# Up weights of an expert in rows of 32 KB, reloaded in one transfer of 4 MB

## The chip, the cores and the metric

The kernel runs on one core of a Trainium2 chip. The metric is the device time of one execution in microseconds; the median of the runs is compared. A profiled execution gives the trace.

## What is computed

Two layers of a diffusion backbone in float32 over 1024 latent tokens and 256 context tokens of width 1024. Layer 0 has neighbourhood attention, layer 1 a bidirectional recurrent block. Each layer ends in a mixture of 32 experts: a router picks 2 of them for every token, and an expert computes

```
hdn = silu(xb @ w1[e]) * (xb @ w3[e])      # w1, w3: 1024 x 512
out = hdn @ w2[e]                          # w2: 512 x 1024
```

Layer 0's experts take all 1280 tokens, layer 1's the 1024 latent ones.

## The kernel before

The change concerns the two expert stages, `experts(0, ...)` and `experts(1, ...)`. The tokens of an expert are cut into items of 32 rows. A **place** is one expert with its items; there are 32 places in an order that mixes full and sparse experts. For every item:

- GpSimd gathers its rows (`gather`, L1697, four buffers `xg`), and VectorE transposes them into `xT` (L1902).
- TensorE does `up` (L1821): 64 matmuls over the chunks 0 to 3 of the expert's weights, which hold w1 and w3.
- ScalarE and VectorE make the hidden rows and transpose them; TensorE does `down` (L1836): 32 matmuls over the chunks 4 and 5, which hold w2.
- ScalarE, or in layer 1 VectorE, moves the result to `y`, and it is stored to `ys_d` from ScalarE's queue (four parts of a buffer).

TensorE's order in a place is `up` of the next item, then `down` of the one before, so at the end of a place the `up` of the next expert's first item stands ahead of the `down` of this expert's last. The last place is done without this overlap.

**Weights.** An expert's weights are six chunks of [128, 2048] float32, 1 MB each, in one of four buffers `wt[b]`, b = place mod 4, 48 KB a partition. The first experts come chunk by chunk (`chunk`, `chunk_at`, L1626, L1631), partly during the stage before. The others are reloads from SP's queue (`reload`, L1643; L1673 for the last buffer's chain): three transfers of 2 MB (L1635), each of two chunks, 128 rows of 16 KB. In HBM, `strips` lays w1 and w3 of an expert out as two blocks of 128 rows of 16 KB and w2 as one.

**Semaphores.** `used[q]` counts the items whose matmuls with chunk q are done. Before a reload of chunks q and q + 1, SP waits for `used[q + 1]` to reach the item count at the end of the place that had the buffer. `w_in[b][q]` tells that a transfer has landed; `arrived` makes TensorE wait for it ahead of chunk 0, 2 and 4 of a place's first item. SP issues in program order, so a wait holds back all issues behind it: the next reload, and after the last one the loads for the merge of the results (L1199, L1464). ScalarE's and GpSimd's transfers have queues of their own, but all queues use the same 16 DMA engines: q1 is SP's, q10 ScalarE's, q0 GpSimd's.

Of the kernel before, what the change touches and what calls it, by code (L numbers as in the profile page):

```python
# [14 lines left out]
P = 128  # L15
D = 1024
# [13 lines left out]
EXPERTS = GROUPS * EPG  # L30
# [6 lines left out]
NCH, CHUNK, WBUF = 6, 2048, 4  # L37
DEEP = 4
SOON = 4
FIXED = WBUF - 1  # L40
# [63 lines left out]
def flat(ap):  # L104
    return ap.rearrange("p a b -> p (a b)")
# [14 lines left out]

def chunk_of(A, l, e, q):

    rows = A["w13"][l, e, q // 2] if q < 4 else A["w2s"][l, e, 0]
    return rows[:, q % 2 * CHUNK:(q % 2 + 1) * CHUNK]


def rows_reversed(ap, rows):
# [4 lines left out]
def program(nc, A, out):  # L132
    root = ExitStack()
    with root:
# [51 lines left out]
        wt = [slot(b)(f"wt{b}", [P, NCH, CHUNK]) for b in range(WBUF)]  # L186
# [631 lines left out]
        class Projection:  # L818
# [72 lines left out]
            def stream(self, sp):  # L891
                l = self.l
                for n in range(2, self.nt):
                    sp.wait_ge(self.sum1_ok, 3 * (n - 2) + 3)
                    self.load_x(sp, n)
                    q = n - 2
                    if q < NCH:
                        view = chunk_of(A, l, 0, q)
                        sp.dma_start(wt[0][:, q, :], view).then_inc(self.w_in[0][q], 16)

                def second(q):
                    view = chunk_of(A, l, 1, q)
                    sp.dma_start(wt[1][:, q, :], view).then_inc(self.w_in[1][q], 16)
# [4 lines left out]
                def third(q):  # L908
                    view = chunk_of(A, l, 2, q)
                    sp.dma_start(wt[2][:, q, :], view).then_inc(self.w_in[2][q], 16)  # L910
# [637 lines left out]
        def experts(l, nt, w_in, merge):  # L1548
# [14 lines left out]
            def T(*shape):  # L1563
# [6 lines left out]
                return ap.rearrange(f"p ({' '.join(names)}) -> p {' '.join(names)}", **dict(zip(names, shape)))  # L1570

            OH, A2, A2c, gl, _, goh, _, _, oh0, oh1, (_, _, _, best0, best1) = scratch(nt)
            in_group = flat(OH[:, 0]).rearrange("p (t g e) -> p t g e", t=nt, g=GROUPS)
            of_group = flat(OH[:, 1])[:, 0:nt * EPG].rearrange("p (t e) -> p t e", t=nt)
            chosen = flat(OH[:, 1])[:, nt * EPG:3 * nt * EPG].rearrange("p (k t e) -> p k t e", k=2, t=nt)
            both = bass.AP(tensor=oh0.tensor, offset=oh0.offset, ap=[list(oh0.ap[0]), [nt * EPG, 2], [EPG, nt], [1, EPG]])
# [24 lines left out]
            used = [nm(f"used{q}") for q in range(NCH)]  # L1601
# [3 lines left out]
            passed, sp_passed = nm("passed"), nm("sp_passed")  # L1605
# [5 lines left out]
            w13v, w2v = A["w13"][l], A["w2s"][l]  # L1611
# [3 lines left out]
            w_in = w_in + [[nm(f"w{FIXED}{q}") for q in range(NCH)]]  # L1615
# [6 lines left out]
            with nc.Block() as block:  # L1622
                @block.sync
                def _(sp):
                    def chunk(e, b, q):
                        sp.dma_start(wt[b][:, q, :], chunk_of(A, l, e, q)).then_inc(w_in[b][q], 16)  # L1626

                    def chunk_at(e, b, q):
                        view = w13v[bass.ds(e, 1), q // 2] if q < 4 else w2v[bass.ds(e, 1), 0]
                        view = view.rearrange("o p c -> (o p) c")[:, q % 2 * CHUNK:(q % 2 + 1) * CHUNK]  # L1630
                        sp.dma_start(wt[b][:, q, :], view).then_inc(w_in[b][q], 16)  # L1631

                    def two_chunks_at(e, b, q):
                        view = w13v[bass.ds(e, 1), q // 2] if q < 4 else w2v[bass.ds(e, 1), 0]
                        sp.dma_start(flat(wt[b][:, q:q + 2, :]), view.rearrange("o p c -> (o p) c")).then_inc(w_in[b][q], 16)  # L1635

                    def reload(r, b):

                        e = sp.value_load(ert[0:1, bass.ds(r, 1)], min_val=0, max_val=EXPERTS - 1)
                        done = sp.value_load(bnd[0:1, bass.ds(r - WBUF + 1, 1)], **span)  # L1640
                        for q in range(0, NCH, 2):
                            sp.wait_ge(used[q + 1], done + (1 if q == NCH - 2 else 0))
                            sp.sem_inc(sp_passed, 1)  # L1643
                            two_chunks_at(e, b, q)

                    for q in Projection.LEFT[l]:
                        chunk(1, 1, q)
                    merge.early_loads(sp)
                    sp.wait_ge(tab_ok, 2)
                    e = sp.value_load(ert[0:1, FIXED:FIXED + 1], min_val=0, max_val=EXPERTS - 1)  # L1650
                    for q in range(4, NCH):
                        chunk_at(e, FIXED, q)
                    sp.wait_ge(e_ok, 1)
                    sp.wait_ge(masks, 4)
                    for q in (2, 3):
                        chunk_at(e, FIXED, q)
                    sp.wait_ge(idx_ok, 2)
                    chunk_at(e, FIXED, 0)
                    sp.wait_ge(masks, 8)
                    chunk_at(e, FIXED, 1)  # L1660
                    sp.wait_ge(tab_ok, 3)
                    with sp.Fori(1, TURNS - 1) as i:
                        for b in range(WBUF):
                            reload(WBUF * i + b, b)
                    for b in range(FIXED):
                        reload(LAST - FIXED + b, b)
                    count = sp.value_load(bnd[0:1, EXPERTS + 2:EXPERTS + 3], min_val=1, max_val=EXPERTS)
                    with sp.Fori(0, count) as k:
                        e = sp.value_load(chain[0:1, bass.ds(k, 1)], min_val=0, max_val=EXPERTS - 1)
                        done = sp.value_load(chain[1:2, bass.ds(k, 1)], **span)  # L1670
                        for q in range(0, NCH, 2):
                            sp.wait_ge(used[q + 1], done + (1 if q == NCH - 2 else 0))
                            sp.sem_inc(sp_passed, 1)  # L1673
                            two_chunks_at(e, FIXED, q)

                    for b, load in enumerate((merge.into_first, merge.into_second, merge.into_third)):
                        r = EXPERTS - WBUF + b + 1
                        done = sp.value_load(bnd[0:1, r:r + 1], **span)
                        sp.wait_ge(used[3], done)
                        sp.sem_inc(sp_passed, 1)  # L1680
                        sp.wait_ge(used[5], done + 1)
                        sp.sem_inc(sp_passed, 1)
                        load(sp)
                    merge.stores(sp)
# [87 lines left out]
                def _(t):  # L1772
# [28 lines left out]
                    def landed(r):  # L1801
                        return past[r % WBUF] + 16 * (r // WBUF) + 16

                    def arrived(b, q, r, more):

                        if q % 2 == 0:
                            t.wait_ge(w_in[b][q], landed(r) if more is None else more + landed(r))
                        elif r < WBUF:
                            t.wait_ge(w_in[b][q], (16 * l if b < FIXED else 0) + 16)
# [501 lines left out]
        def weights_in():  # L2311

            return [[root.enter_context(nc.semaphore(f"w{b}{q}")) for q in range(NCH)] for b in range(FIXED)]

        hT, OT = at("hT", MODS_AT, [P, KD, N]), at("OT", OT_AT, [P, KD, N])
        w_in = weights_in()
# [19 lines left out]
def strips(w1, w3, w2):  # L2336

    up = lambda w: np.asarray(w).reshape(2, EXPERTS, 4, 8, 32, 4, P).transpose(0, 1, 3, 2, 4, 5, 6)
    both = np.stack((up(w1), up(w3)), axis=-2)
    w13 = both.reshape(2, EXPERTS, 2, 4, P, D).transpose(0, 1, 2, 4, 3, 5)  # L2340
    dn = np.asarray(w2).reshape(2, EXPERTS, 4, 4, 32, D).transpose(0, 1, 3, 2, 4, 5)
    w2s = dn.reshape(2, EXPERTS, 1, 4, P, D).transpose(0, 1, 2, 4, 3, 5)
    return {"w13": np.ascontiguousarray(w13).reshape(2, EXPERTS, 2, P, 2 * CHUNK),
            "w2s": np.ascontiguousarray(w2s).reshape(2, EXPERTS, 1, P, 2 * CHUNK)}


# [70 lines left out]
```

## Time and profile before

| | |
|---|---|
| median of 3 runs | 2678.44 us (2677.75 to 2681.88) |
| the profiled execution's own time | 2678.04 us |
| its span, first to last instruction | 2675.9 us |
| TensorE busy (matmul) | 2486.5 us, 93% |
| VectorE, ScalarE, GpSimd busy | 45%, 26%, 17% |
| HBM read, written | 575.27 MB, 61.95 MB |
| mean granted TensorE clock | 0.963 |

Busy shares are averages over stages with different limits. The two expert stages lie at about 1008 to 1513 us and 2135 to 2628 us of the span. A time "from A to B" is in microseconds from the span's start.

### The profile page before, as it was taken

What the parts mean: (1) busy time and instruction counts of PE and PEld (TensorE: products, weight loads), DVE (VectorE), ACT (ScalarE), POOL (GpSimd) and SP (SyncE); (2) the same over time, 40 slices, a digit from 0 to 9 for tenths busy, and PEclk for the clock granted to TensorE, in tenths of its full rate; (3) what the DMA queues carried; (4) which work ended last, traced back from release to release, by engine and by line L of the source; (5) the groups of instructions that cost most, each with busy time, mean ns of one, the idle gap of its engine ahead of it and who ended that gap; (6) DMA issues with size and microseconds to landing.
All of it is one profiled execution on the core that took longest, in us unless ns stands there. A gap on an engine that the chain in (4) does not pass through costs nothing. (4 is left out here: it accounts for less than half of the span.)

```text
span 2675.9 us, 63251 instructions
## 1 busy us (share of the span) xinstructions
PE 2486.5 (93%) x26162; PEld 1781.2 (67%) x26162; DVE 1212.0 (45%) x2794; ACT 690.3 (26%) x1427; POOL 460.8 (17%) x554
## 2 busy tenths in 40 slices
PE   7999999999989969999999679999999699999994
PEld 6887788788854546777777474554545478996552
DVE  3234333333454473222222256565575655554545
ACT  4223222323230002333333364345330000000002
POOL 0012112111122102222222220000011022222222
PEclk9999999999999979999999889999999799999997
DMA  6323223223163469999999761011045799999997
GB/s 272 118 90 122 87 100 119 85 94 125 48 245 120 142 255 408 391 421 420 421 420 421 294 238 32 32 34 45 0 161 202 294 406 420 420 420 421 422 421 285
DMA packets 102664, 633.75 MB, mean 237 GB/s; under 512 B 17016, under 2 KB 29788, under 8 KB 68048
## 3 DMA queue, kind: packets, MB, share of 16 engines
q1 hardware_dynamic: 70768, 539.65, 50.4%
q0 software_dynamic: 17024, 48.27, 4.8%
q10 hardware_dynamic: 14688, 43.08, 4.1%
q8 instruction: 151, 2.47, 0.4%
q14 instruction: 33, 0.27, 0.0%
HBM read 575.27 MB, written 61.95 MB: 238 GB/s over the span
## 5 line engine op out<-in xcount | busy, mean ns | idle before, releaser
L1821 PE MATMUL PS<-wt,xT 128*32 128x256 f32 x11648 | 688.1, 384 | 25.0 <-DMA wt<-in_w 19.0
L1821 PEld LDWEIGHTS PS<-wt,xT 128*32 128x32 f32 x11648 | 494.6, 111 | 173.8 <-issue 27.1
L1836 PE MATMUL PS<-wt,hidT 128*32 128x256 f32 x5824 | 364.4, 382 | 9.5 <-issue 7.5
L1836 PEld LDWEIGHTS PS<-wt,hidT 128*32 128x32 f32 x5824 | 250.7, 111 | 81.9 <-issue 12.2
L731 PE MATMUL PS<-hT,slab 128*128 128x256 f32 x1280 | 295.8, 385 | 6.3 <-DVE low L624 3.5
L1902 DVE STREAM_TRANSPOSE xT<-xg 128x256 f32<-128x256 f32 x186 | 82.8, 445 | 458.2 <-PE PS L1821 450.6
L731 PEld LDWEIGHTS PS<-hT,slab 128*128 128x128 f32 x1280 | 239.7, 192 | 42.8 <-issue 6.5
L444 POOL TENSOR_SCALAR prob<-prob,inv 128x640 f32<-128x640 f32 (+2 forms) x80 | 130.3, 1629 | 661.6 <-DVE inv L639 661.6
L1738 ACT ACTIVATE u<-PS 128x128 f32<-128x128 f32 x186 | 51.7, 278 | 684.1 <-PE PS L1821 670.1
L1697 POOL DMA_INDIRECT xg<-h_d,ib x192 | 198.8, 1035 | 163.8 <-POOL ib L1694 160.4
L522 ACT ACTIVATE prob<-prob,low 128x640 f32<-128x640 f32 (+2 forms) x160 | 117.5, 735 | 300.2 <-DVE low L624 300.2
L624 DVE CUSTOM_DVE_ANT_0 prob<-PS,tab 128x640 f32<-128x640 f32 (+2 forms) x160 | 108.5, 716 | 184.4 <-PE PS L760 178.2
L1746 ACT ACTIVATE y<-PS 32x256 f32<-32x256 f32 x384 | 144.2, 375 | 140.3 <-PE PS L1836 136.8
L736 PE MATMUL PS<-slab,hT 128*128 128x128 f32 x1280 | 151.6, 277 | 0.0
L1923 DVE TENSOR_TENSOR y<-PS,RL 32x256 f32<-32x256 f32 x356 | 148.8, 418 | 5.6
L736 PEld LDWEIGHTS PS<-slab,hT 128*128 128x128 f32 x1280 | 146.4, 192 | 3.9 <-issue 2.4
L940 POOL TENSOR_TENSOR xt_p<-xt_p,bg_p 128x1024 f32<-128x1024 f32 x18 | 44.8, 2495 | 583.7 <-DVE bg_p L982 431.2
L1694 POOL COPY ib<-idx 128x1 int32 (+1 forms) x192 | 35.3, 184 | 635.4 <-DVE xT L1902 599.1
L1078 PE MATMUL PS<-wo,OT 128*128 128x512 f32 x320 | 144.1, 604 | 0.0
L2268 PE MATMUL PS<-uT,wg 128*128 128x512 f32 (+1 forms) x384 | 138.9, 521 | 1.4 <-issue 1.4
L2268 PEld LDWEIGHTS PS<-uT,wg 128*128 128x128 f32 x384 | 72.9, 190 | 69.6 <-issue 66.7
L1914 DVE STREAM_TRANSPOSE hidT<-hid 128x128 f32<-128x128 f32 x184 | 57.4, 312 | 134.4 <-PE PS L1836 133.9
(313 smaller groups left out, 2773.9 us busy)
## 6 DMA issues: line engine op xcount, KB each, us to landing
wt<-in_w SPq DMA_DIRECT2D x112, 2048.0 KB
wt<-in_w2s SPq DMA_DIRECT2D x56, 2048.0 KB
aw<-in_ada_w SPq DMA_DIRECT2D x48, 1024.0 KB, 5.0
wt<-in_w SPq DMA_DIRECT2D x32, 1024.0 KB, 8.3
ys_d<-y ACTq DMA_DIRECT2D x184, 128.0 KB, 6.3
wt<-in_w2s SPq DMA_DIRECT2D x16, 1024.0 KB, 11.9
slab<-in_slabs SPq DMA_DIRECT2D x24, 512.0 KB, 3.4
tab<-in_tables SPq DMA_DIRECT2D x8, 1408.0 KB, 7.2
```

What stands on the lines that cost most here:

```text
L444: g.tensor_scalar(x, x, inv[:, b, 1:2], None, ALU.mult).then_inc(pg_ok, 1)
L522: a.activation(x, x, ACT.Exp, scale=-1.0, bias=low[:, b, j:j + 1], accum_out=sums[:, b, j:j + 1]).then_inc(exp_ok, 1)
L624: v.tensor_tensor_reduce(prob[b][:, j, lo:640], S[j][:, lo:640], tab[h % 2][:, j, at:at + 640 - lo], 1.0, 3e38, ALU.add, ALU.min, low[:, b ...
L731: mm = pe.matmul(W[HALF[n]], slab[m][:, k, :], hT[:, k, c * PW:(c + 1) * PW], start=(k == 0), stop=(k == KD - 1))
L736: mm = pe.matmul(W[HALF[n]][:, o * P:(o + 1) * P], hT[:, k, c * PW + o * P:c * PW + (o + 1) * P], slab[2][:, k, :], start=(k == 0), stop=( ...
L1078: mm = t.matmul(PS[:, self.banks[n % 2] + h, :], self.Z[:, k, n * P:(n + 1) * P], self.wo[:, k, h * 512:(h + 1) * 512], start=(k == 0), st ...
L1697: g.indirect_dma_start(out=xg[j][:, :], out_offset=None, in_=h2v, in_offset=bass.IndirectOffsetOnAxis(ap=ib[:, j:j + 1], axis=0), bounds_c ...
L1746: ins = a.activation(y[rows, q * QD:q * QD + QD], PS[STRIP * q:STRIP * q + STRIP, DOWN, 0:QD], ACT.Copy)
L1821: mm = t.matmul(PS[32 * g:32 * g + 32, UP, 0:QD], xT[:, k * 32:k * 32 + 32], wt[b][:, q, c * 1024 + g * QD:c * 1024 + g * QD + QD], start= ...
L1836: mm = t.matmul(PS[32 * g:32 * g + 32, DOWN, 0:QD], hT_[:, k * 32:k * 32 + 32], wt[b][:, q, c * 1024 + g * QD:c * 1024 + g * QD + QD], sta ...
L1923: ins = v.tensor_tensor(y[rows, q * QD:q * QD + QD], PS[strip, DOWN, 0:QD], merge.gate[strip, :], ALU.mult)
L2268: mm = t.matmul(dst[:, c:c + wd], wg[:, q, k, o * P:(o + 1) * P], uT[k][:, c:c + wd], start=(k == 0), stop=(k == 1))
```

## The change

`strips` lays w1 and w3 of an expert out as one block of 128 rows of 32 KB. A reload has two transfers: chunks 0 to 3 in one of 4 MB (`up_at`), issued when `used[3]` has reached the count, and chunks 4 and 5 in one of 2 MB (`down_at`), as before. TensorE waits for a landing ahead of chunk 0 and chunk 4 only (`arrived`); the first loads into a buffer keep a transfer and a wait for each chunk, now with rows of 8 KB out of rows of 32 KB. The same bytes are moved.

```diff
--- before.py
+++ after.py
@@ -120,8 +120,8 @@
 
 def chunk_of(A, l, e, q):
 
-    rows = A["w13"][l, e, q // 2] if q < 4 else A["w2s"][l, e, 0]
-    return rows[:, q % 2 * CHUNK:(q % 2 + 1) * CHUNK]
+    rows, first = (A["w13"][l, e, 0], 0) if q < 4 else (A["w2s"][l, e, 0], 4)
+    return rows[:, (q - first) * CHUNK:(q - first + 1) * CHUNK]
 
 
 def rows_reversed(ap, rows):
@@ -1626,22 +1626,28 @@
                         sp.dma_start(wt[b][:, q, :], chunk_of(A, l, e, q)).then_inc(w_in[b][q], 16)
 
                     def chunk_at(e, b, q):
-                        view = w13v[bass.ds(e, 1), q // 2] if q < 4 else w2v[bass.ds(e, 1), 0]
-                        view = view.rearrange("o p c -> (o p) c")[:, q % 2 * CHUNK:(q % 2 + 1) * CHUNK]
+                        view, first = (w13v[bass.ds(e, 1), 0], 0) if q < 4 else (w2v[bass.ds(e, 1), 0], 4)
+                        view = view.rearrange("o p c -> (o p) c")[:, (q - first) * CHUNK:(q - first + 1) * CHUNK]
                         sp.dma_start(wt[b][:, q, :], view).then_inc(w_in[b][q], 16)
 
-                    def two_chunks_at(e, b, q):
-                        view = w13v[bass.ds(e, 1), q // 2] if q < 4 else w2v[bass.ds(e, 1), 0]
-                        sp.dma_start(flat(wt[b][:, q:q + 2, :]), view.rearrange("o p c -> (o p) c")).then_inc(w_in[b][q], 16)
+                    def up_at(e, b):
+                        view = w13v[bass.ds(e, 1), 0]
+                        sp.dma_start(flat(wt[b][:, 0:4, :]), view.rearrange("o p c -> (o p) c")).then_inc(w_in[b][0], 16)
+
+                    def down_at(e, b):
+                        view = w2v[bass.ds(e, 1), 0]
+                        sp.dma_start(flat(wt[b][:, 4:6, :]), view.rearrange("o p c -> (o p) c")).then_inc(w_in[b][4], 16)
 
                     def reload(r, b):
 
                         e = sp.value_load(ert[0:1, bass.ds(r, 1)], min_val=0, max_val=EXPERTS - 1)
                         done = sp.value_load(bnd[0:1, bass.ds(r - WBUF + 1, 1)], **span)
-                        for q in range(0, NCH, 2):
-                            sp.wait_ge(used[q + 1], done + (1 if q == NCH - 2 else 0))
-                            sp.sem_inc(sp_passed, 1)
-                            two_chunks_at(e, b, q)
+                        sp.wait_ge(used[3], done)
+                        sp.sem_inc(sp_passed, 1)
+                        up_at(e, b)
+                        sp.wait_ge(used[5], done + 1)
+                        sp.sem_inc(sp_passed, 1)
+                        down_at(e, b)
 
                     for q in Projection.LEFT[l]:
                         chunk(1, 1, q)
@@ -1668,10 +1674,12 @@
                     with sp.Fori(0, count) as k:
                         e = sp.value_load(chain[0:1, bass.ds(k, 1)], min_val=0, max_val=EXPERTS - 1)
                         done = sp.value_load(chain[1:2, bass.ds(k, 1)], **span)
-                        for q in range(0, NCH, 2):
-                            sp.wait_ge(used[q + 1], done + (1 if q == NCH - 2 else 0))
-                            sp.sem_inc(sp_passed, 1)
-                            two_chunks_at(e, FIXED, q)
+                        sp.wait_ge(used[3], done)
+                        sp.sem_inc(sp_passed, 1)
+                        up_at(e, FIXED)
+                        sp.wait_ge(used[5], done + 1)
+                        sp.sem_inc(sp_passed, 1)
+                        down_at(e, FIXED)
 
                     for b, load in enumerate((merge.into_first, merge.into_second, merge.into_third)):
                         r = EXPERTS - WBUF + b + 1
@@ -1803,7 +1811,7 @@
 
                     def arrived(b, q, r, more):
 
-                        if q % 2 == 0:
+                        if q % 4 == 0:
                             t.wait_ge(w_in[b][q], landed(r) if more is None else more + landed(r))
                         elif r < WBUF:
                             t.wait_ge(w_in[b][q], (16 * l if b < FIXED else 0) + 16)
@@ -2337,10 +2345,10 @@
 
     up = lambda w: np.asarray(w).reshape(2, EXPERTS, 4, 8, 32, 4, P).transpose(0, 1, 3, 2, 4, 5, 6)
     both = np.stack((up(w1), up(w3)), axis=-2)
-    w13 = both.reshape(2, EXPERTS, 2, 4, P, D).transpose(0, 1, 2, 4, 3, 5)
+    w13 = both.reshape(2, EXPERTS, 1, 8, P, D).transpose(0, 1, 2, 4, 3, 5)
     dn = np.asarray(w2).reshape(2, EXPERTS, 4, 4, 32, D).transpose(0, 1, 3, 2, 4, 5)
     w2s = dn.reshape(2, EXPERTS, 1, 4, P, D).transpose(0, 1, 2, 4, 3, 5)
-    return {"w13": np.ascontiguousarray(w13).reshape(2, EXPERTS, 2, P, 2 * CHUNK),
+    return {"w13": np.ascontiguousarray(w13).reshape(2, EXPERTS, 1, P, 4 * CHUNK),
             "w2s": np.ascontiguousarray(w2s).reshape(2, EXPERTS, 1, P, 2 * CHUNK)}
```

## Rows read from the trace of the kernel before

**Rows 1.** The page's 40 equal slices of the span, 66.9 us each

```profile
PE   7999999999989969999999679999999699999994
DMA  6323223223163469999999761011045799999997
```

**Rows 2.** Windows of 50 us in the two expert stages, with the columns' names

```profile
core 0: us, PE busy (x) PEld busy (x) DVE busy (x) ACT busy (x) POOL busy (x), PEclk, DMA share, GB/s
1150.00:1200.00 50.00, 50.00 (x936) 39.95 (x931) 12.18 (x40) 17.15 (x49) 11.97 (x20) 1.00 1.01 420
2300.00:2350.00 50.00, 50.00 (x934) 45.05 (x927) 28.83 (x78) 2.78 (x10) 11.14 (x19) 1.00 1.01 420
2550.00:2600.00 50.00, 44.89 (x764) 25.01 (x760) 23.89 (x64) 2.22 (x8) 9.74 (x16) 0.90 1.01 422
```

**Rows 3.** Waits (us, times, longest): TensorE 2150 to 2600, VectorE 1030 to 1480

```profile
PE PS L1821 <- DMA wt<-in_w: 19.0, 7, 4.2
...
DVE xT L1902 <- PE PS L1821: 270.3, 87, 3.2
```

**Rows 4.** The page's DMA issues of the whole execution

```profile
wt<-in_w SPq DMA_DIRECT2D x112, 2048.0 KB
wt<-in_w2s SPq DMA_DIRECT2D x56, 2048.0 KB
...
ys_d<-y ACTq DMA_DIRECT2D x184, 128.0 KB, 6.3
```

**Rows 5.** Timeline of SP's queue in layer 1's expert stage (start us, us)

```profile
2127.67 12.69 SPq L1631 DMA_DIRECT2D wt<-in_w  x4
2143.82 2.07 SPq L1635 DMA_DIRECT2D wt<-in_w  x2
...
2222.63 2.05 SPq L1635 DMA_DIRECT2D wt<-in_w  x2
```

**Rows 6.** Timeline of TensorE in layer 1's expert stage

```profile
2141.61 3.66 PE L1821 MATMUL PS<-wt,xT 128*32 128x256 f32 x64 [1.52 <-DVE hid L1910]
...
2570.53 1.91 PE L1836 MATMUL PS<-wt,hidT 128*32 128x256 f32 x32
2575.89 3.64 PE L1821 MATMUL PS<-wt,xT 128*32 128x256 f32 x32 [3.44 <-DMA wt<-in_w]
2581.20 3.64 PE L1821 MATMUL PS<-wt,xT 128*32 128x256 f32 x32 [1.67 <-DMA wt<-in_w]
2584.61 2.15 PE L1836 MATMUL PS<-wt,hidT 128*32 128x256 f32 x32
...
2617.27 4.65 PE L1821 MATMUL PS<-wt,xT 128*32 128x256 f32 x64
```

**Rows 7.** The chain of waits between 2400 and 2620

```profile
2538.30 42.85 DMA wt<-in_w
```

**Rows 8.** Windows of single stretches, columns as in rows 2

```profile
1106.00:1108.00 2.00, 2.00 (x44) 1.57 (x37) 0.28 (x1) 1.47 (x4) 0.83 (x1) 1.00 0.07 17
...
2145.00:2146.00 1.00, 1.00 (x28) 0.71 (x21) 0.61 (x2) 0.28 (x1) 0.04 (x1) 1.00 0.68 131
...
2581.20:2584.60 3.40, 3.40 (x32) 1.57 (x36) 0.00 (x0) 0.00 (x0) 0.00 (x0) 0.50 1.00 424
```

**Rows 9.** DMA queues, 1137 to 1460: packets, MB, share of 16 engines

```profile
q1 hardware_dynamic: 8256, 120.15, 88.3%
q10 hardware_dynamic: 3011, 8.25, 6.5%
q0 software_dynamic: 3002, 7.06, 5.7%
```

**Rows 10.** DMA queue of SP, 1107.8 to 1460 and 2143.8 to 2581.2

```profile
q1 hardware_dynamic: 8955, 130.54, 88.1%
...
q1 hardware_dynamic: 11289, 164.14, 89.3%
```

## The prediction

> **What bounds the kernel now.** I read the page's slices first [rows 1]: the 16 DMA engines are full in two stretches, slices 15 to 21 and 30 to 39, where TensorE is full too. These are the two expert stages, 28 reloads of 6 MB and some 90 items each. The windows part them [rows 2]. In layer 0 (1150 to 1200) TensorE is busy 50.00 of 50.00 us at full clock; the DMA engines are full as well, but nobody waits. In layer 1, 2300 to 2350 looks the same, yet 2550 to 2600 has TensorE at 44.89 of 50 us, clock 0.90, with the DMA still full. The waits name the loads [rows 3]: seven times, 19.0 us. So layer 0 is paced by TensorE, while layer 1 is paced by weight transfers until its last stall, and by TensorE from there to the end.
>
> That last stall is the hinge. TensorE finishes a `down` begun at 2570.53, gets the first 2 MB of the next expert at 2575.89, the second at 2581.20, and never waits for weights again [rows 6]. The chain of waits shows that the second transfer was issued 42.85 us before it landed [rows 7]: the queue is then far behind its issues, so when SP issues it doesn't matter, only how fast the queue moves. Counting from the first reload at 2143.82 [rows 5], the two halves are the ups of the 26th reload, 78 - 1 = 77 transfers of 2.097 MB = 161.5 MB.
>
> **The change part by part.** The sum is made against the profiled execution's 2678.04 us (span 2675.9 and 2.1 around it), 0.4 us under the median run.
>
> *Packets.* A weight transfer is 128 rows of 16 KB. With rows of 32 KB, the up weights need 128 packets fewer, and one set of 16 completions fewer: 144 packets an expert, 9 per engine. What does a packet cost besides its bytes? Two queues with different packet sizes over the same 323 us of 16 engines (5168 engine-us) [rows 9]: q1 has 8256 packets, 120.15 MB, 88.3% = 4563 us; q10 has 3011 packets, 8.25 MB, 6.5% = 336 us. With time = a x packets + b x bytes these give b = 0.0373 us per KB (thousand bytes) and a = 9.2 ns (8.2 to 10.3 within the rounding of 6.5%). Nine packets x 9.2 ns = 0.083 us an expert, and x 26 experts until the hinge **-2.2 us**. Bounds: 0, if a row of 32 KB is still moved as two packets; -4.4, twice the estimate, because q10 writes to HBM and q1 reads, so the fit is coarse.
>
> The Trainium skill ("DMA: Bandwidth & Descriptors", section on why small descriptors are slow) gives a fixed cost of some 3 cycles per packet and calls merging worth it only at small sizes; the trace's 9.2 ns has the same sign, and the rule by itself would make this term nearly nothing, the case without a gain below.
>
> *The first issue comes later.* Before, the first half of the reload waits for used[1], half of a place's last `up`; now all of it waits for used[3], the end. An `up` is 64 matmuls in 3.66 us, so this is 1.8 us later. Queued behind it on SP is only the down reload, whose own wait is later still. Where the queue has work this costs nothing: the sixth reload of layer 1 is issued at 2222.63 [rows 5], when q1 still has to move what is left of five reloads; the queue moves 0.375 MB per us [rows 10], so 31.5 MB issued from 2143.8 last until about 2228, and 1.8 us fit into the 5. But at the stage's start nothing is queued: SP issues the first reload at 2143.82, the previous load (1 MB) was issued about 2140, the first item's `up` began at 2141.61, and in 2145 to 2146 the DMA share is 0.68 [rows 8]. All of the 1.8 us is then lost to a stage paced by the queue: **+1.8 us** (bounds 0, if the gap was there anyway, and 2.0).
>
> *The wait at the hinge is coarser.* Before, half of the `up` was done when the second 2 MB landed; the rest took 2581.20 to 2584.61, 3.4 us, at the low clock (0.50) [rows 6, 8]. Now 64 matmuls start at that landing. At the low clock throughout they take 6.8 us; if the clock returns after the 3.4 us in which it was low before, the other half takes 1.7 us. Hence +1.7 to +3.4. TensorE has now been idle since 2572.4 without the half `up` in between, but at 2584.61 the clock was back 3.4 us after the resumption, so I take the near end: **+1.8 us**. The earlier stalls get the same delay and hide it: TensorE then arrives later at the next stall, which ends by the queue's time. Behind the hinge the next weights are early: the last expert's `up` at 2617.27 waits for no load [rows 6].
>
> *Layer 0.* The queue runs dry once, at 1106 to 1108 (share 0.07) [rows 8], since TensorE frees the buffers late; there the reload now starts 1.8 us later too. Does TensorE ever wait because of it? The tightest place is late in the stage: 21 reloads after the gap, an `up` begins at 1468.21, and its 4 MB are complete when 20 x 6.29 + 4.19 = 130.0 MB have moved since 1107.8. The queue has moved 130.5 MB at 1460 [rows 10]. The slowest of 16 engines lags the mean: at the hinge, 164.1 MB had moved for 161.5 MB needed (plus at most 1.0 MB left from before), 1.6 to 2.6 MB, 4 to 7 us. So the margin is 1 to 4 us; 1.8 us later and 21 x 0.083 = 1.7 us quicker leaves it. **0** (bound: +2 where it is just gone).
>
> *Others' transfers.* The gathers of rows and the stores of results share the engines with weights: q0 and q10 have about 3000 packets for 63 items, 48 an item, 3 per engine [rows 9]. If each waits for one whole weight packet, now 1.22 us in place of 0.61 (32.8 and 16.4 thousand bytes at b), an item's three take 3 x 1.22 and some own time, about 4.5 us, under the item's 5.18 us. The store takes 6.3 us to land [rows 4]; + 3 x 0.61 = 8.1 us, and its buffer is wanted again four items, 20 us, later. DVE has never waited for a gather [rows 3]. Cost nothing; without that cover, see the rivals. SP's fewer instructions and TensorE's fewer waits: nothing, neither is waited for.
>
> The sum: -2.2 + 1.8 + 1.8 + 0 = **+1.4 us**, 2679.4 against the profiled 2678.04, and **2679.8 us** against the median. All terms at their low bounds: -4.4 + 0 + 1.7 = -2.7, 2675.7. All high: 0 + 2.0 + 3.4 + 2 = +7.4, 2685.8.
>
> **Rivals.** *No gain from packets.* A row of 32 KB is cut in two, or a packet's fixed part overlaps its bytes: +1.8 + 1.8 = +3.6, 2682.0. For it: the DMA share is 1.01 and 420 GB/s with rows of 16 KB already, with little room above. Against it: the fit's 9.2 ns.
>
> *Slower: long rows move more slowly.* The 16 engines read rows 32 KB apart in place of 16 KB, and each holds on to a row for 1.22 us; if that costs 2% of the rate, 26 reloads x 16.8 us (437.4 us from first issue to hinge / 26) = 437 us give 8.7 us more in layer 1, and in layer 0 21 x 16.8 x 2% = 7.1 us against a margin of about 2.5 us, some 5 us. With +3.6 this is +17, 2696. It decides (over 0.2%, 5.4 us) from 0.4% on. Against it: rows of 16 KB flow at the same 420 GB/s in every window. The Trainium skill ("DMA: Bandwidth & Descriptors", the row on HBM row pitch in "Latency and other measured facts") has the rate falling with large power-of-two pitches, 207 in place of 214 GB/s at 512 KB, and says nothing as low as 32 KB; by 3% everywhere the same sum would be +23.
>
> *Slower: gathers late.* If small packets wait for two weight packets each, 3 x 2.44 = 7.3 us an item exceeds 5.18, and some 140 items in full-queue stretches x 2.1 us are +300 us. It decides from 1.7 us of waiting per packet. Against it: the store's 6.3 us, about what three single turns and a landing need.
>
> *Faster: the laggard catches up.* A transfer lands with its slowest engine, 4 to 7 us behind the mean at the hinge. If fewer, longer packets halve that (3 us), the sum is -1.6, 2676.8; with the large packet gain -3.8 or, with no loss at the start, -5.6, 2672.8. Nothing in the profile says why an engine lags, so it may as well grow.
>
> **How the numbers follow.** Forecast 0.55, no gain from packets 0.18, long rows slower 0.13 (a third of it under 0.4%), gathers late 0.02, laggard 0.12 (two thirds still within the bound). 0.2%, 5.4 us, is about what a measurement of this kernel tells from no change. Faster 0.06 (0.04 from the laggard, 0.02 from the forecast's own low side), slower 0.13 (0.09 long rows, 0.02 gathers, 0.02 high sums), same 0.81; the laggard growing takes 0.03 more to slower and the unexpected 0.02 to faster: 0.08, 0.76, 0.16. The range takes in the bounds 2675.7 and 2685.8, the laggard's side down to 2674 and part of the slower rival, up to 2687.
>
> **What would show it.** Right: 56 issues of 4096 KB; q1's packets fewer by 56 x 144 = 8064; stalls on `up` of layer 1 with 64 matmuls behind one landing; the last stall ending at 2581 + 1.8 - 2.2, near 2581; TensorE in layer 0 still without a wait; stores landing in about 8 us. Wrong: an unchanged packet count (no gain), GB/s under 417 in full windows or a hinge after 2587 (long rows, laggard), DVE waiting for gathers, or a first gap in layer 1 that doesn't widen.

## The result, and the profile after

The changed kernel takes 2683.11 us (median of 20 runs, 2676.52 to 2687.82), the kernel before, on the same chip, 2677.37 (20 runs, 2674.16 to 2683.26). The ratio is 1.0019, with a 95% interval from 1.0012 to 1.0025: +5.1 us (3.2 to 6.7). The forecast was +1.4 us, 2679.8. The time lies in the range, on the slow side, and at the edge of the 0.2% called "no change".

The page of the profile after: the slices of rows 1, q1's row, and the issues of rows 4 (times issued, size, median us to landing).

```profile
PE   7999999999989969999999579999999699998984
...
DMA  6323223223163469999999761111045799999996
...
q1 hardware_dynamic: 62704, 539.65, 50.0%
...
wt<-in_w SPq DMA_DIRECT2D x56, 4096.0 KB, 31.0
...
ys_d<-y ACTq DMA_DIRECT2D x184, 128.0 KB, 7.9
```

56 issues of 4096 KB stand in the place of 112 of 2048 KB. q1 had 70768 packets before; 62704 are 8064 fewer, as forecast. The store takes 7.9 us to land, 6.3 before [rows 4], 8.1 forecast.

The windows after, columns as in rows 2:

```profile
1150.00:1200.00 50.00, 50.00 (x931) 35.29 (x929) 11.28 (x37) 17.52 (x49) 10.93 (x18) 1.00 1.01 425
2300.00:2350.00 50.00, 50.00 (x929) 45.57 (x925) 29.21 (x79) 2.65 (x10) 12.14 (x20) 1.00 1.00 421
2550.00:2600.00 50.00, 42.81 (x748) 28.57 (x744) 22.25 (x60) 2.22 (x8) 8.68 (x15) 0.90 1.01 424
2581.90:2585.30 3.40, 3.36 (x32) 1.83 (x36) 0.00 (x0) 0.00 (x0) 0.00 (x0) 0.50 1.04 447
2585.30:2588.50 3.20, 3.20 (x44) 1.82 (x40) 0.05 (x1) 0.15 (x1) 0.00 (x0) 0.67 1.03 435
```

The DMA engines move 421 to 425 GB/s, 420 to 422 before [rows 2]: the long rows are not slow. In 2550 to 2600 TensorE is busy 2.1 us less. The timeline of TensorE in layer 1 after (L1829 is `up`, L1844 `down`; L1821 and L1836 before):

```profile
2136.97 2.36 PE L1829 MATMUL PS<-wt,xT 128*32 128x256 f32 x20
...
2581.94 6.35 PE L1829 MATMUL PS<-wt,xT 128*32 128x256 f32 x64 [7.19 <-DMA wt<-in_w]
2588.10 1.92 PE L1844 MATMUL PS<-wt,hidT 128*32 128x256 f32 x32
...
2618.08 3.62 PE L1844 MATMUL PS<-wt,hidT 128*32 128x256 f32 x32 [2.16 <-issue]
```

The stage's first `up` starts at 2136.97 (2134.98 before), so the times are best read from there. The hinge comes 444.97 us after it, 446.22 before. From the hinge to the `down` at 2618.08 it takes 36.14 us, 33.64 before (2581.20 to 2614.84). At the hinge all 64 matmuls now stand behind one landing, and they need 2581.94 to 2588.10, 6.2 us: by the windows the clock is at 1.2 GHz (0.50) for the first 3.4 us and still 0.67 on the mean of the next 3.2.

At the stage's start, the timeline of SP's queue after, and the windows around it:

```profile
2147.54 0.33 SPq L1635 DMA_DIRECT2D wt<-in_w  x1
```

```profile
2146.00:2147.00 1.00, 1.00 (x24) 0.76 (x20) 0.00 (x0) 0.00 (x0) 0.92 (x1) 1.00 0.22 71
2147.00:2148.00 1.00, 1.00 (x27) 0.71 (x20) 0.65 (x2) 0.28 (x1) 0.07 (x1) 1.00 0.03 1
```

The first reload is issued 10.57 us after the first `up`, 8.84 before [rows 5], and the DMA engines run empty (share 0.22, then 0.03; 0.68 before [rows 8]).

In layer 0 TensorE waits for no weights, yet it waits. The waits of PEld (TensorE's weight loads, LDWEIGHTS) and of PE (its matmuls) in 1026 to 1500 after (us, times, longest); the same view of before has no line for TensorE at all:

```profile
PEld PS L1844 <- issue: 2.1, 2, 1.5
...
PE PS L1844 <- issue: 1.1, 1, 1.1
```

and one such place in the timeline after (PE and PEld):

```profile
1146.89 1.50 PE L1844 MATMUL PS<-wt,hidT 128*32 128x256 f32 x22
...
1149.44 0.81 PE L1844 MATMUL PS<-wt,hidT 128*32 128x256 f32 x9 [1.06 <-issue]
1149.45 0.54 PEld L1844 LDWEIGHTS PS<-wt,hidT 128*32 128x32 f32 x9 [1.54 <-issue]
```

"issue" is idle time for which the profile shows nothing that was waited for. This one falls behind the 22nd of the 32 matmuls of a `down`, where the program has no wait: `down` waits ahead of its first and its 17th matmul at most.

To size this I sum, in 1026 to 1500, by how much the time from one item's first transpose to the next exceeds the usual 5.18 us; this is called the excess: 0.4 us before, 3.3 after.

The profiled spans (2675.9 and 2680.6 us, +4.7) fall apart thus, from the first `up` to the end of the last `down` of each expert stage:

| | before | after | difference |
|---|---|---|---|
| start to layer 0's first `up` | 1008.22 | 1007.83 | -0.4 |
| layer 0's experts | 504.67 | 506.75 | +2.1 |
| between the expert stages | 622.09 | 622.39 | +0.3 |
| layer 1's experts | 493.18 | 495.07 | +1.9 |
| the rest | 47.74 | 48.56 | +0.8 |

The middle part differs by up to 4.4 us between the profiles of kernels that don't differ there (621.8 to 626.3 in this study), so single spans say little below 0.2%. The last `down` of a stage is in these lengths, and its clock varies: in layer 0 it took 3.34 us in before, 1.93 in after and 3.59 in after_again. To its start, layer 0 is 3.5 us longer in after and 2.7 in after_again, and layer 1 is 1.2 and 1.9 us longer. What follows compares the parts of profiles with one another, and whole times by the timed runs.

### The profile page after: what moved, and what is told of

Read it like the earlier page. It is cut to its first block and busy times, and to the rows that moved or that the text cites. A ratio compares the mean times of both kernels' runs of the same rounds, so it can differ in the third digit from the quotient of the medians.

```text
span 2680.6 us, 63027 instructions
## 1 busy us (share of the span) xinstructions
PE 2485.7 (93%) x26162; PEld 1791.2 (67%) x26162; DVE 1211.5 (45%) x2794; ACT 690.3 (26%) x1427; POOL 461.2 (17%) x554
## 3 DMA queue, kind: packets, MB, share of 16 engines
q1 hardware_dynamic: 62704, 539.65, 50.0%
## 5 line engine op out<-in xcount | busy, mean ns | idle before, releaser
L1829 PE MATMUL PS<-wt,xT 128*32 128x256 f32 x11648 | 704.9, 384 | 28.0 <-DMA wt<-in_w 21.0
L1829 PEld LDWEIGHTS PS<-wt,xT 128*32 128x32 f32 x11648 | 508.5, 111 | 165.5 <-issue 38.4
L1844 PE MATMUL PS<-wt,hidT 128*32 128x256 f32 x5824 | 381.9, 382 | 10.4 <-issue 8.3
L1844 PEld LDWEIGHTS PS<-wt,hidT 128*32 128x32 f32 x5824 | 261.7, 111 | 82.8 <-issue 13.0
```

The source lines that it names most:

```text
L1829: mm = t.matmul(PS[32 * g:32 * g + 32, UP, 0:QD], xT[:, k * 32:k * 32 + 32], wt[b][:, q, c * 1024 + g * QD:c * 1024 + g * QD + QD], start= ...
L1844: mm = t.matmul(PS[32 * g:32 * g + 32, DOWN, 0:QD], hT_[:, k * 32:k * 32 + 32], wt[b][:, q, c * 1024 + g * QD:c * 1024 + g * QD + QD], sta ...
```

## The experiments

Three parts of the change (the late first issue, the coarse wait, the longer rows) were done alone or left out; then sizes on either side; then versions meant to keep only what helps. The parts, in us (L1 is layer 1's length as in the table above; "to hinge" counts from the stage's first `up` to the landing that ends the last wait for weights):

| kernel | ratio to before, 95% | excess, layer 0 | to hinge | hinge to next-to-last `down` | L1 |
|---|---|---|---|---|---|
| before | | 0.4 | 446.2 | 33.6 | 493.2 |
| after | 1.0012 to 1.0025 | 3.3 | 445.0 | 36.1 | 495.1 |
| after_again | 1.0006 to 1.0023 | 2.7 | 445.7 | 36.1 | 495.7 |
| e1: late first issue | 1.0004 to 1.0022 | 0.9 | 447.8 | 34.4 | 494.7 |
| e2: coarse wait | 0.9998 to 1.0016 | 0.7 | 446.2 | 35.5 | 494.6 |
| e3: 4 MB, rows of 16 KB | 1.0010 to 1.0027 | 0.4 | 447.4 | 36.3 | 497.7 |
| e4: rows of 8 KB | 1.0011 to 1.0029 | 0.4 | 450.1 | 33.6 | 497.1 |
| e6: after, split | 0.9991 to 1.0009 | 3.6 | 443.6 | 33.4 | 490.5 |
| e8: rows of 48 KB | 1.0102 to 1.0133 | 20.1 | 455.8 | 36.0 | 505.6 |
| e9: short, then long | 0.9984 to 1.0002 | 0.7 | 443.7 | 33.3 | 490.6 |
| e9_again | 0.9980 to 0.9998 | 1.3 | 443.7 | 33.4 | 490.5 |
| e10: quarters | 0.9979 to 0.9997 | 1.6 | 444.0 | 32.5 | 489.7 |

**after_again: the changed kernel once more**, beside e1, e2 and e3 on one chip.

> The changed kernel once more, to see which parts of its profile repeat. Theory: four parts, in its first profile: TensorE short of instructions three times in layer 0 (0.6, 0.4 and 1.4 us, at starts of places, while the fetch of the next code block stood behind weight packets of 32 KB), the first reload of layer 1 issued 1.8 us later, the queue then 3 us quicker up to the last stall, and the up behind that stall longer (6.2 in place of 3.4 us, all at the low clock). If so, the same three gaps stand at the same instructions, and the total is 4 to 6 us above the kernel before. Rival: the gaps and the clock are chance; then they stand elsewhere, and what repeats is only the last stall's coarser wait, some 2 to 3 us.

2681.78 us against 2677.50, ratio 1.0015 (1.0006 to 1.0023), +4.0 us. Layer 1 is 2.5 us longer, layer 0's excess 2.3 us larger, and the break in the `down` near 1148 is there again, after the same 22 matmuls:

```profile
1148.10 0.81 PE L1844 MATMUL PS<-wt,hidT 128*32 128x256 f32 x9 [0.44 <-issue]
```

The other breaks repeat only in part, which the expectation had otherwise: the one near 1141 is there again (0.2 us of PEld), the one near 1066 is not, and others stand at 1052, 1059, 1252 and 1259.

**e1_late_issue: only the later issue of the first half.**

```diff
-    sp.wait_ge(used[q + 1], done + (1 if q == NCH - 2 else 0))
+    sp.wait_ge(used[max(q + 1, 3)], done + (1 if q == NCH - 2 else 0))
```

> The kernel before, with only one wait moved: the first 2 MB of a reload waits for used[3] in place of used[1]; layout, rows of 16 KB, three transfers and TensorE's waits as before. Theory (queue-paced layer 1, dry at its start): first reload of layer 1 issued 1.8 us later, the last stall of layer 1 ends 1.5 to 2 us later, total +1.8 us. Rival (the gap at the start is there anyway, or the queue makes it up): stall's end unchanged, total 0 to +0.3 us.

The timeline of TensorE of e1, first `up` and hinge:

```profile
2132.59 4.93 PE L1821 MATMUL PS<-wt,xT 128*32 128x256 f32 x64
...
2580.37 3.64 PE L1821 MATMUL PS<-wt,xT 128*32 128x256 f32 x32 [3.55 <-DMA wt<-in_w]
```

447.78 us to the hinge, +1.6, and L1 +1.5. What is lost at the stage's start arrives whole at its end. The timed ratio, 1.0013, would be +3.5 us, of which the profile accounts for 1.5 and 0.5 of excess; its interval begins at +1.1. The stretch behind the hinge is 0.8 us longer than in before, though nothing in it was changed: the `down` behind the last half `up` took 2.88 us, 2.15 before [rows 6], at a clock of 0.64 on the mean. So one such stretch is good to about 1 us.

**e2_coarse_wait: only the coarser wait.** Ahead of chunk 0 TensorE waits for both halves.

```diff
-    if q % 2 == 0:
-        t.wait_ge(w_in[b][q], landed(r) if more is None else more + landed(r))
+    for p in {0: (0, 2), 2: (), 4: (4,)}[q]:     # q even
+        t.wait_ge(w_in[b][p], landed(r) if more is None else more + landed(r))
```

> The kernel before, with TensorE waiting for both halves of the up weights ahead of chunk 0; transfers and their issue as before. Theory: the last stall of layer 1 ends with the same landing (2581 us within 1), and behind it 64 matmuls in place of 32 at the low clock: last down 2.5 to 3.4 us later, total +2.5 to +3.4 us; layer 0 unchanged. Rival (the clock is back half way): +1.7 us. Rival (the wait costs nothing, since later weights are late too): 0.

The timeline of TensorE of e2 at the hinge (first `up` at 2136.30):

```profile
2582.46 5.74 PE L1822 MATMUL PS<-wt,xT 128*32 128x256 f32 x64 [7.57 <-DMA wt<-in_w]
2588.01 1.91 PE L1837 MATMUL PS<-wt,hidT 128*32 128x256 f32 x32
```

The hinge is where it was (446.16), as the forecast had it for the earlier stalls, and behind it 1.9 us are lost. The `up` takes 5.6 us, not the 3.4 + 1.7 of the forecast. 1.9 us is less than the 2.5 to 3.4 expected and nearer to the rival's 1.7 (the clock back half way); the timed ratio, 1.0007, does not tell it from no change.

**e3_one_4mb_short_rows: the change without the longer rows.** One transfer of 4 MB, of 256 rows of 16 KB.

```diff
-    view = w13v[bass.ds(e, 1), 0]
-    sp.dma_start(flat(wt[b][:, 0:4, :]), view.rearrange("o p c -> (o p) c")).then_inc(w_in[b][0], 16)
+    view = w13v[bass.ds(e, 1)].rearrange("o h p c -> (o p) h c")
+    sp.dma_start(flat(wt[b][:, 0:4, :]).rearrange("p (h c) -> p h c", h=2), view).then_inc(w_in[b][0], 16)
```

> The changed kernel with one part undone: weights laid out as before and moved in one transfer of 4 MB of 256 rows of 16 KB; issue, waits and TensorE's code as in the changed kernel. Theory (a row's length counts twice, as 9 ns a packet saved and as a longer turn for code fetches): no stall for instructions in layer 0 at the three places, so layer 0 ends 2 to 3 us earlier than in the changed kernel; in layer 1 the last stall ends 2 to 3 us later than in it. Total about that of the changed kernel, +4 to +5 us over before. Rival (no cost of a packet): stall's end as in the changed kernel, total +2. Rival (TensorE's code placement alone makes the stalls): the three gaps stay.

The timeline of TensorE of e3 at the hinge (first `up` at 2138.92):

```profile
2586.35 6.46 PE L1829 MATMUL PS<-wt,xT 128*32 128x256 f32 x64 [7.61 <-DMA wt<-in_w]
2592.62 1.92 PE L1844 MATMUL PS<-wt,hidT 128*32 128x256 f32 x32
```

447.43 us to the hinge, 2.5 more than in the profile of after and 1.8 more than in after_again, 2.1 on the mean. e3 differs by 8 packets per engine and expert: 8 x 9.2 ns x 26 = 1.9 us. So a row of 32 KB does save its packet. The excess in layer 0 is 0.4, and TensorE has no wait there: with TensorE's instructions unchanged, short rows take the breaks away. The whole is no better than after (1.0018), since layer 1 loses what layer 0 gets back.

**e4_rows_8kb: the kernel before with twice the packets for the up weights.**

```diff
-    w13 = both.reshape(2, EXPERTS, 2, 4, P, D).transpose(0, 1, 2, 4, 3, 5)
+    w13 = both.reshape(2, EXPERTS, 2, 2, 2, P, D).transpose(0, 1, 2, 3, 5, 4, 6)
...
-    sp.dma_start(flat(wt[b][:, q:q + 2, :]), view.rearrange("o p c -> (o p) c")).then_inc(w_in[b][q], 16)
+    sp.dma_start(wt[b][:, q:q + 2, :], view.rearrange("o h p c -> (o p) h c")).then_inc(w_in[b][q], 16)
```

> The kernel before with the up weights laid out and reloaded in rows of 8 KB: the same three transfers of 2 MB, the same waits and issues, but 256 packets more an expert, 16 per engine. Theory (a packet costs 9 ns beside its bytes): the last stall of layer 1 ends 16 x 9.2 ns x 26 = 3.8 us later, counted from TensorE's first up of the layer (446.2 us before); items of layer 0 as before or smoother. Rival (the fixed part is hidden, and the changed kernel's faster queue came from the 4 MB transfer as such): 446.2 within 0.5.

The timeline of TensorE of e4:

```profile
2138.32 1.93 PE L1828 MATMUL PS<-wt,xT 128*32 128x256 f32 x16
...
2588.46 3.64 PE L1828 MATMUL PS<-wt,xT 128*32 128x256 f32 x32 [1.92 <-DMA wt<-in_w]
```

and its queue of SP in 1137 to 1460:

```profile
q1 hardware_dynamic: 12961, 118.75, 88.6%
```

The timed ratio is 1.0020, +5.4 us (2.9 to 7.8). 450.14 us to the hinge, +3.9, where 16 x 9.2 ns x 26 are 3.8. In the same stretch of layer 0 the queue moves 118.75 MB, 1.2% less than with 8256 packets [rows 9]. The price of a packet holds on both sides of 16 KB.

**e8_rows_48kb: the step carried on.** All weights of an expert in one block of 128 rows of 48 KB, one transfer of 6 MB, issued when `used[5]` allows it, one wait ahead of chunk 0.

```diff
-    sp.wait_ge(used[3], done)
-    up_at(e, b)
-    sp.wait_ge(used[5], done + 1)
-    down_at(e, b)
+    sp.wait_ge(used[5], done + 1)
+    sp.dma_start(flat(wt[b][:, 0:6, :]), view.rearrange("o p c -> (o p) c")).then_inc(w_in[b][0], 16)
```

> A stronger dose: a whole expert as rows of 48 KB in one transfer of 6 MB, issued when the down is done too, one wait ahead of chunk 0. Theory (a code fetch waits for the row in front of it): the short stalls of TensorE for code in layer 0's places (3.3 and 2.7 us in the two profiles of the changed kernel, 0.4 before) grow to 5 us or more; the stage in layer 1 is longer by the issue's further 1.7 us and by 2 MB more ahead of the last stall's end, 5 us, less 1 us for packets. Total +10 to +16 us. Rival (placement of the code): stalls of 3 us or less.

2710.26 us, ratio 1.0118 (4 runs), +31 us, twice what was expected. The waits of e8 in 1026 to 1500 (us, times, longest), and its issues in 1137 to 1460:

```profile
DVE xT L1903 <- DMA xg<-h_d,ib: 52.0, 13, 4.8
PEld PS L1822 <- issue: 12.1, 23, 5.1
PEld PS L1822 <- DVE xT L1903: 7.9, 8, 1.3
PE PS L1822 <- DMA wt<-in_w: 4.7, 1, 4.7
```

```profile
ys_d<-y ACTq DMA_DIRECT2D x61, 128.0 KB, 14.3
xg<-h_d,ib POOLq DMA_INDIRECT x62, 16.5
```

Layer 0 has 19.7 us more excess than before and layer 1 is 12.4 us longer. Item by item, the excess of layer 0 has three parts of much the same size:

- Some 7.6 us are one stall for weights at 1065.75, which now come in 6 MB at once: 4.67 us of waiting and an `up` of 6.43 us at the low clock. The 5.1 us of "issue" of PEld are this same stall.
- Some 7 us lie in 1255 to 1331 and 1474 to 1497, where VectorE waits for the gathers and TensorE for VectorE's `xT`. A gather takes 16.5 us to land and a store 14.3, in after 9.0 and 8.1 in the same stretch.
- Some 5 us are breaks like those of after. In the timeline of TensorE of e8 one stands again behind 22 matmuls of a `down`:

```profile
1157.12 0.81 PE L1837 MATMUL PS<-wt,hidT 128*32 128x256 f32 x9 [0.76 <-issue]
```

The breaks are thus about as large as the expectation had them. The stall for weights and the late gathers in layer 0 it had not counted.

**e6_split_first_and_last: the change, with the 4 MB cut in two 2 MB transfers where the halves matter.** Rows stay 32 KB apart in HBM; places 4, 28, 29 and 30 take columns 0 to 1 and 2 to 3 apart, each after its own `used`, and TensorE waits for each.

```diff
+SPLIT = [4, 28, 29, 30]
...
+    if halves:
+        for q in (0, 2):
+            sp.wait_ge(used[q + 1], done)
+            half_at(e, b, q)
```

> The changed kernel, but four reloads of a layer (the first and the last three before the chain) move their up weights as two halves of 2 MB (rows of 16 KB out of the 32 KB), issued on used[1] and used[3] and waited for apart, as in the kernel before. Theory: first reload 1.8 us earlier than in the changed kernel and TensorE's half up back at the last stall, so layer 1 is 1.5 to 1.8 + 2.5 = 4 us shorter than in it (495.1, 495.7 us), 491 to 492; layer 0 keeps its 2 to 3 us of short stalls for code; total 0 to +2 us over before. Rival (the coarse wait's price is the clock's chance): 493 to 494.

Two places of TensorE's timeline of e6 in layer 1:

```profile
2137.39 1.93 PE L1846 MATMUL PS<-wt,xT 128*32 128x256 f32 x16
...
2580.98 3.62 PE L1846 MATMUL PS<-wt,xT 128*32 128x256 f32 x32 [3.56 <-DMA wt<-in_w]
2584.37 1.96 PE L1861 MATMUL PS<-wt,hidT 128*32 128x256 f32 x32
```

443.59 us to the hinge, 33.4 behind it, L1 490.5: layer 1 gives 2.7 us in place of losing 2. But layer 0 is 507.8 us long, 3.1 more than before, with breaks near 1066, 1148 and 1259, and the whole comes out even, ratio 1.0000. The waits of e6 in layer 0 look like those of after:

```profile
PEld PS L1846 <- issue: 2.1, 2, 1.3
PEld PS L1861 <- issue: 1.0, 2, 0.6
```

**e9_short_then_long: e6, with layer 0 in halves throughout**, so in rows of 16 KB.

```diff
+    halves = halves or not l
...
-    if q % 4 == 0:
+    if q % 4 == 0 or (q == 2 and not l):
```

> A version put together from the findings: weights laid out in rows of 32 KB; layer 0, paced by TensorE, reloads and waits in halves of 2 MB (rows of 16 KB) as before; layer 1, paced by the queue, reloads 4 MB in rows of 32 KB, except for the first and the last three before the chain, which come in halves. Theory: layer 0 as before (no stalls for code), layer 1 at 491 to 492 in place of 493.2 us; total -1 to -2 us against before. Rival (halves cut out of 32 KB rows move more slowly than whole rows of 16 KB): layer 0 gets waits for weights, total above before.

2675.13 us, ratio 0.9993 (0.9984 to 1.0002). Excess 0.7, layer 0 503.6 us, L1 490.6.

**e9_again**, on another chip, beside e10.

> The version of e9 once more, on another occasion, since its first ratio (0.9993, 0.9984 to 1.0002) doesn't tell it from the kernel before. Theory: layer 1 again at 490 to 491 us against 493.2, layer 0 without stalls for code, ratio 0.999. Rival (the first profile was luck): layer 1 at 493, ratio 1.000.

Ratio 0.9989 (0.9980 to 0.9998): -3 us, and L1 490.5 once more. Its hinge in the timeline of TensorE (first `up` at 2137.53):

```profile
2581.24 3.20 PE L1853 MATMUL PS<-wt,xT 128*32 128x256 f32 x32 [3.57 <-DMA wt<-in_w]
```

**e10_quarters: e9, with the up weights of places 28 to 30 of layer 1 in four transfers of 1 MB**, each with its wait.

```diff
+QUARTERS = [28, 29, 30]
...
+    for q in range(4):
+        sp.wait_ge(used[q], done)
+        quarter_at(e, b, q)
```

> As e9, but in layer 1 the up weights of the last three reloads before the chain come in four transfers of 1 MB (rows of 8 KB), each issued and waited for by itself. Theory: when the last of them lands, only 16 matmuls of the up are left in place of 32, 1.7 us less at the low clock or 0.9 at the full one; packets cost 32 per engine x 9 ns = 0.3 us at most. Layer 1 at 489 to 490 us, total 1 us under e9. Rival (TensorE, held up four times, is at the low clock for longer, or small transfers land later): no gain, or 1 us over e9.

2674.59 us, ratio 0.9988 (0.9979 to 0.9997). The last wait now has only 16 matmuls behind it:

```profile
2582.11 1.93 PE L1865 MATMUL PS<-wt,xT 128*32 128x256 f32 x16 [1.42 <-DMA wt<-in_w]
```

L1 is 489.7, 0.9 us less than e9's and 0.8 less than e9_again's. The timed runs can't tell it from e9: each interval holds the other's median ratio.

## Why the prediction was off by 3 to 4 us, step by step

*Packets, -2.2: right.* e3 against after gives 2.1 us for the 128 rows (1.9 by the forecast's price), e4 3.9 for 3.8. The rival without a gain (2682.0) is the nearest to the median by number, but not by cause.

*The first issue comes later, +1.8: right.* e1 gives +1.6 to the hinge; e3, which has it too, +1.2.

*The wait at the hinge is coarser, +1.8: the mechanism right, the term too small.* It measured 2.5 in both profiles of after, 1.9 in e2 and 2.6 in e3; in the kernels that keep two halves the stretch stays at 33.3 to 34.4. I had let the clock return 3.4 us after TensorE resumed, as in [rows 6]. But there TensorE had already worked on a half `up` from 2575.89 within that stall; now it had stood idle for 7.19 us, and the `up` took 6.2 us, near the bound of 6.8. The row had been read without what TensorE did ahead of it.

With these three, the forecast for layer 1 is +1.4. Measured are 1.2 and 1.9 to the start of the last `down`: the hinge moved by -1.3 and -0.6, and 2.5 came behind it. The whole layer, 1.9 and 2.5, has 0.6 us more, because the last `down` took 3.55 and 3.53 us, 2.90 before; e9_again had it in 2.81 and e4 in 2.98, e3 in 3.60, and no experiment says why.

*Layer 0, "**0**": the step that failed.* It asked only whether weights come late, and they don't. What came was 2.3 to 2.9 us of breaks in TensorE's own stream of instructions. That the length of the rows causes them is shown: e3 has the same instructions on TensorE and rows of 16 KB, and no break; e4 (8 KB) has none; e6 with rows of 32 KB has them near the same places as the two profiles of after; e8 with 48 KB has about 5 us of them. Kernels with rows of 16 KB have 0 to 1.2 us above before's 0.4, so the effect does not begin from nothing at 32 KB.

What comes late is read from a queue that the prediction's list of others' transfers left out. In 1137 to 1460 the trace after has a queue of instructions on the same 16 engines, with packets of 16 KB:

```profile
q1 hardware_dynamic: 5550, 121.01, 88.2%
...
q8 instruction: 27, 0.44, 0.6%
```

The trace before has 26 in that stretch, and every profile of this study has 151 in all, so its packets can be paired by number. Their times stand in the traces, one packet after the other. In the profiles with rows of 32 KB (after, after_again, e6), all 13 breaks of PEld in layer 0 (of 0.15 us or more, in 1026 to 1500) end 1.3 to 2.2 us behind the end of a q8 packet, and such packets are some 7 us apart. The packet ahead of the break behind the 22nd matmul is number 66. It can be set against the same item's `down` in all twelve profiles (us; the packet's end is counted from the start of that `down`, and breaks count from 0.1 us):

| profile | rows in layer 0 | packet's end | break of PEld |
|---|---|---|---|
| before, e1, e2, e3, e4, e9 | 16 KB, e4 8 KB | -1.0 to -0.5 | none |
| e10 | 16 KB | -0.15 | 0.12 |
| e9_again | 16 KB | 0.02 | 0.44 |
| e6 | 32 KB | 0.07 | 0.56 |
| after_again | 32 KB | 0.49 | 0.93 |
| e8 | 48 KB | 0.74 | 1.25 |
| after | 32 KB | 1.13 | 1.54 |

Where the packet comes later, the break is longer by as much; in after it runs from 1147.06 to 1148.01, in before from 1143.70 to 1144.77, against `down`s that start at 1146.89 and 1145.32. So these breaks are waits for TensorE's code, which lands late among long rows. What holds the packet back (the rows in front of it on its DMA engine, or a later request) no run separates.

The Trainium skill fits this reading in two places. "DMA: Bandwidth & Descriptors", section on queues, rings and completion order, has each engine finish a whole packet of one queue before it turns to the next; its packet is a group of some 9 to 17 descriptors, and whether a row here is one is not shown. "Runtime: NRT & Kernel Launch", section on instruction fetch, has an engine's code refilled in blocks of 16 KiB by its own queue, at a cost "mostly hidden". The traces agree with the second: q8's packets are of 16 KB, and of its 40 packets in 1026 to 1500 of after three have a break behind them.

*Others' transfers, 0: right as far as it went.* Stores land in 7.9 us (8.1 forecast), and VectorE does not wait for a gather in after. The cover was counted for the data queues only. At 48 KB it is gone for the gathers as well.

The sum as measured: layer 0 +2.5 (2.1 and 2.9 by the two lengths, 2.9 and 2.3 by the excess), layer 1 +2.2, together 4.7 against 5.1 and 4.0 timed. The 0.8 us behind the last stage lie in the merge of the results, whose first four matmuls of L1515 took 3.62 us in after and 2.78 in before; e1, without the coarse wait, has them too (3.48), and e2, with it, has not (2.53), so they don't belong to the change. That the time fell into the range is in part luck: the high side had +2 for weights that come late in layer 0, which did not happen, and nothing for code.

Three slips in the working change no term. Slices 30 and 31 of the DMA row stand at 5 and 7 tenths, so the second full stretch begins with slice 32. The `up` at 2141.61 is the stage's second; the first begins at 2134.98. And 3% of the rate by the sum of the second rival are 3.6 + 13.1 + 8.1, nearly +25, not +23.

*The rivals.* Long rows at a lower rate: excluded, 421 to 425 GB/s and a hinge that came earlier. Gathers late: excluded at 32 KB; at 48 KB it happens, with 52.0 us of VectorE's waits for gathers and some 7 us of excess. The laggard: with the packets' -2.1, -0.2 for the set of completions and the first issue's +1.6 the hinge should move by -0.7; it moved by -1.3 and -0.6; nothing of the size of 3 us is left for it in either direction.

## What to carry to other kernels

A merged transfer saves packets on a queue that sets the pace, but it pays at the two ends of the stage: at the first reload, where nothing is queued, and at the last wait, where all the work behind the landing runs at a clock that the wait itself has lowered. Merge in the middle, split at the ends, and price the work behind a wait at the low clock unless the engine worked shortly before. Where TensorE is the bound, a load gains nothing by long rows and may lose: look at every queue on the DMA engines, that of instructions too, before calling another queue's longer turn free; here short rows in layer 0 and long ones in layer 1 turn +5 us into -2 to -3, of which the first measurement alone is not clear of no change.

## What the runs showed of the hardware that was not expected

- Breaks in TensorE's instruction stream grow with the row length of another queue's transfers. In 1026 to 1500, above before's excess of 0.4 us: nothing at 8 KB, 0 to 1.2 us at 16 KB, 2.3 to 3.2 at 32 KB, some 5 at 48 KB. At one and the same instruction, the break in twelve profiles follows the landing of one packet of the instruction queue, up to 1.54 us for one that ended 1.13 us into the `down`.
- Small transfers beside long rows land later. A gather takes 7.1 us beside rows of 8 KB (e4), 7.3 beside 16 KB (e9_again), 9.0 beside 32 KB (after) and 16.5 beside 48 KB (e8); a store of 128 KB takes 6.1, 6.4, 8.1 and 14.3 (1137 to 1460). In e8 all weights have the long rows, in after only the up weights.
- A packet of a read from HBM costs 9 to 10 ns beside its bytes, whether rows of 8, 16 or 32 KB are compared: 2.1 us for 208 packets per engine (e3 against after), 3.9 for 416 (e4 against before).
- After 7.2 us without work the clock stayed at 1.2 GHz through nearly all of a 64-matmul `up`, 6.2 us (5.6 to 6.3 us in e2, e3, e8 and after_again, behind waits of 6.7 to 7.6). After a wait with half an `up` in it, the second half took 3.4 us and the `down` behind it 2.15 [rows 6], 2.9 in e1 and 2.0 in e6.
